# A decoder layer with 32 experts: low halves on VectorE, logits from the raw residual, choice by match-and-replace, first gather ahead of the loop

## The reference, cut to what matters

```python
x = x + hybrid_mixer(rms_norm(x, norm_mix), w_in, ...)      # z = h @ w_in, five column groups of 1024
#   pool: sliding means minus the token, per-group matmul, w_pool_proj
#   lru: width-4 conv, gates (sigmoid), associative scan over the tokens, * gelu(z_gelu), w_lru_proj
#   m = sigmoid(g_a) * y_a + sigmoid(g_b) * y_b;  m @ w_mix_out
memn = rms_norm(mem, norm_mem)
x = x + cross_attention(rms_norm(x, norm_xattn), memn, w_q, w_kv, w_o)
xn = rms_norm(x, norm_moe).reshape(256, 1024)
logits = xn @ w_router + b_router                            # 256 x 32
top_val, top_idx = lax.top_k(logits, 4)
gates = softmax(top_val)
# each expert e: hact = clamped_swiglu(xb @ w_gate_up[e] + b_gate_up[e]); hact @ w_down[e] + b_down[e]
x = x + sum over the chosen experts of gate * expert(xn)
out = rms_norm(x, norm_final)
```

## Time and profile before

| | |
|---|---|
| median of three runs | 1324.38 us |
| profiled execution | 1324.83 us |
| its span, first to last instruction | 1323.0 us |
| mean granted clock of TensorE, share of full | 0.977 |
| TensorE busy | 1204.0 us (91%) |
| VectorE busy | 485.9 us (37%) |
| ScalarE busy | 249.0 us (19%) |
| GpSimd busy | 238.5 us (18%) |
| read from HBM | 459.74 MB, mean 348 GB/s |
| chain that ended last | DMA 51%, PE 41%, DVE 4%, ACT 1% |

### The profile page before, as it was taken

How to read it: one execution, slowest core, us unless ns; L and a number is a source line. 1 busy time by engine, 2 the same in 40 slices (tenths; PEclk the granted TensorE clock), 3 DMA queues, 4 the chain that set the end, 5 groups by cost and what they waited for, 6 DMA issues and landing times.

```text
span 1323.0 us, 18583 instructions
## 1 busy us (share of the span) xinstructions
PE 1204.0 (91%) x7545; PEld 626.3 (47%) x7545; DVE 485.9 (37%) x705; ACT 249.0 (19%) x347; POOL 238.5 (18%) x73
## 2 busy tenths in 40 slices
PE   6996999999969999998899999988999999989996
PEld 6996999998733333333333333333333333333332
DVE  6995976313223322232222222322222223222224
ACT  5427644535320100001000000000000000000002
POOL 5843786976230000000000000000000000000000
PEclk9997989999868999999999999999999999999999
DMA  7533453644968999999999999999999999999991
GB/s 283 188 123 141 146 220 135 220 171 147 350 247 356 429 428 428 429 428 429 429 428 429 428 429 429 429 428 429 429 428 428 429 428 429 428 428 429 429 428 79
DMA packets 36527, 461.25 MB, mean 349 GB/s; under 512 B 4224, under 2 KB 4240, under 8 KB 5392
## 3 DMA queue, kind: packets, MB, share of 16 engines
q1 hardware_dynamic: 36000, 459.82, 83.7%
q0 software_dynamic: 208, 0.54, 0.1%
q10 hardware_dynamic: 288, 0.45, 0.1%
HBM read 459.74 MB, written 1.05 MB: 348 GB/s over the span
## 4 chain that ended last, share of the span: by engine, by line
DMA 51%; PE 41%; DVE 4%; ACT 1%; issue 1%; SPq 0%; DVEq 0%; ACTq 0%
DMA late<-in_w_gate_up 50%; PE ps L1181 17%; PE ps L1064 4%; PE ps L1065 4%; PE ps L1066 4%; PE ps L1083 2%; PE ps L1085 2%; PE ps L1084 2%; PE ps L1099 2%; DVE act_lo L689 1%; PE ps L1232 1%; DVE s L781 1%; PE ps L1206 1%; DMA raw<-in_dense 1%; PE ps L1240 1%
## 5 line engine op out<-in xcount | busy, mean ns | idle before, releaser
L1181 PE MATMUL ps<-late,s 128*64 128x512 f32 x1128 | 517.0, 601 | 65.9 <-DMA late<-in_w_gate_up 64.9
L1182 PE MATMUL ps<-late,s 128*64 128x512 f32 x1128 | 517.0, 601 | 0.0
L1181 PEld LDWEIGHTS ps<-late,s 128*64 128x64 f32 x1128 | 144.0, 137 | 393.5 <-issue 256.3
L370 POOL TENSOR_TENSOR wlo<-raw,whi 128x2048 fp32r<-128x2048 f32 x47 | 225.6, 4812 | 116.1 <-ACT whi L449 116.1
L959 DVE TENSOR_TENSOR res<-res,ps 128x1024 f32<-128x1024 f32 x66 | 80.6, 1221 | 266.7 <-PE ps L1232 266.6
L1064 PE MATMUL ps<-act_hi,whi 128*128 128x256 f32 x576 | 165.5, 287 | 6.8 <-issue 4.6
L1065 PE MATMUL ps<-act_lo,whi 128*128 128x256 f32 x576 | 164.9, 286 | 0.0
L1066 PE MATMUL ps<-act_hi,wlo 128*128 128x256 f32 x576 | 164.7, 286 | 0.0
L1182 PEld LDWEIGHTS ps<-late,s 128*64 128x64 f32 x1128 | 144.0, 137 | 0.0
L598 ACT ACTIVATE s<-ps 128x512 f32<-128x512 f32 x64 | 34.7, 594 | 574.6 <-PE ps L1182 574.6
L1181 PE MATMUL ps<-raw,s 128*64 128x512 f32 x272 | 123.9, 598 | 0.0
(11 more groups left out here) (176 smaller groups left out, 1116.0 us busy)
## 6 DMA issues: line engine op xcount, KB each, us to landing
late<-in_w_gate_up SPq DMA_DIRECT2D x125, 2048.0 KB, 25.5
raw<-in_w_down SPq DMA_DIRECT2D x32, 2048.0 KB, 25.6
raw<-in_dense SPq DMA_DIRECT2D x51, 1024.0 KB, 4.8
late<-in_w_down SPq DMA_DIRECT2D x16, 2048.0 KB, 25.3
s<-in_w_down SPq DMA_DIRECT2D x16, 2048.0 KB, 25.3
raw<-in_w_gate_up SPq DMA_DIRECT2D x2, 2048.0 KB, 8.2
s<-in_w_gate_up SPq DMA_DIRECT2D x1, 2048.0 KB, 13.5
res<-in_x SPq DMA_DIRECT2D x2, 512.0 KB, 5.1
```

Source lines behind the costliest of these rows:

```text
L370: nc.gpsimd.tensor_tensor(wlo[m % SPL][:, :], raw[:, n % RAW, :], whi[m % SPL][:, :].bitcast(F32), ALU.subtract)\
L1181: nc.tensor.matmul(ps[0:SLOTS, bank, :], x_tile, lower, start=start, stop=stop)
L1182: return nc.tensor.matmul(ps[SLOTS:P, bank, :], x_tile, upper, start=start, stop=stop)
```

## The change

1. GpSimd makes no low half of a chunk any more. VectorE makes all 48, each at a place written out in its list (`low_weights(name, j)`: all low halves up to chunk j of that matrix).
2. The last transpose reads the residual itself. The norm's factor `rstd` is applied to the logits when they leave PSUM; the gain goes into the router weights (one multiply on GpSimd). The router weights are the stationary operand (32 columns), in four column tiles of the array, two k-tiles into each; the four partial sums are added by a matmul with four stacked unit matrices (`fold`), which also turns them back.
3. The choice: `match_replace` overwrites the four largest (the other four of the eight are set to a value that is absent), and `pick16` is where the result differs from the logits. `place_or_no` is rank + 1 or 0.
4. `gmat` is made on VectorE from the exponentials of all logits, inside the loop's first round. The three bfloat16 parts are made tile by tile, scaled in the same instruction.
5. `select(0, 0)` stands ahead of the loop on TensorE and VectorE, and ahead of the reading of the number of rounds. The router's three loads stand behind the wait for branch B (`yb_done`) with no low halves ahead of them.

```diff
-            for m, n in enumerate(SPLIT_CHUNKS):                       # GpSimd
...
-                nc.gpsimd.tensor_tensor(wlo[m % SPL][:, :], raw[:, n % RAW, :],
-                                        whi[m % SPL][:, :].bitcast(F32), ALU.subtract)
...
+            nc.gpsimd.tensor_tensor(router_w, router_w, moe_gain, ALU.mult).then_inc(S["router_scaled"], 1)
...
+            square(6, res[:, 0, :], xn_rows[:, 0, :], added_up(0))      # ScalarE
+            high_rows(0)
+            for j in range(3):
+                evacuate("xnT", j, lambda j, b: nc.scalar.activation(
+                    xn_f[:, 2 * j:2 * j + 2, :], two(b), ACT.Copy).then_inc(S["freed_act"], 1))
+            middle_rows(0)
+            evacuate("logitT", 0, lambda j, b: nc.scalar.activation(
+                logit_t, b[:, 0:T], ACT.Copy).then_inc(S["freed_act"], 1))
+            square(7, res[:, 1, :], xn_rows[:, 1, :], added_up(1))
+            high_rows(1)
+            middle_rows(1)
...
+            def low_weights(name, j):                                   # VectorE
+                last = SPLIT_CHUNKS.index(DENSE[name] + j)
+                while next_low[0] <= last:
+                    m = next_low[0]
+                    dve.wait_ge(S["dense_hi_ready"], m + 1)
+                    V.tensor_tensor(wlo[m % SPL][:, :], raw[:, SPLIT_CHUNKS[m] % RAW, :],
+                                    whi[m % SPL][:, :].bitcast(F32), ALU.subtract).then_inc(S["dense_lo_ready"], 1)
+                    next_low[0] += 1
...
             for j in range(4):
                 evacuate("lp", j, merge)
-                if j:
-                    low_of(m_f, "merged", j - 1)
-            low_of(m_f, "merged", 3)
+                low_weights(*(("lp", 3), ("mix", 0), ("mix", 1), ("mix", 2))[j])
+                low_of(m_f, "merged", j)
...
+            for j in range(3):
+                evacuate("o", j, onto_residual)
+            inverse_root(0)
+            evacuate("o", 3, onto_residual)
+            rest_rows_of(0)
+            evacuate("xnT", 3, copied(xn_f))
+            low_rows(0)
+            inverse_root(1)
...
+            link(*[V.match_replace(without[:, t, :], top8[:, 8 * t:8 * t + 8], logit[:, t, :], 2 * ABSENT / 3)
+                   for t in both])
+            V.tensor_tensor(pick16[:], without[:, :, 0:EXPERTS], logit[:, :, 0:EXPERTS], ALU.not_equal)\
+                .then_inc(S["picked"], 1)
+            rest_rows_of(1)
...
-            transposed("xnT", xn_rows, 3)                               # TensorE
+            transposed("xnT", res, lambda t: (S["freed_dve"], evacuated(UNIT["o"] + 2 * t + 1)[1]))
...
+            for kk in range(2):
+                for g in range(GROUPS):
+                    k = 2 * g + kk
...
+                    last = nc.tensor.matmul(b[g * EXPERTS:(g + 1) * EXPERTS, 0:T], router_w[:, k, :], xn_f[:, k, :],
+                                            start=kk == 0, stop=kk == 1)
...
+            pe.wait_ge(S["part_hi"], TT)
+            pe.wait_ge(S["part_mid"], TT)
+            pe.wait_ge(S["part_low"], TT)
+            select(0, 0)
             pe.wait_ge(S["freed_dve"], evacuated(NUNIT - 1)[1])
-            pe.wait_ge(S["part_hi"], 3)
             n = needed_rounds(pe)
             with pe.Fori(0, n) as r:
-                select(r, 0)
                 input_ready(r, 0)
```

More of the change, by code:

```diff
@@ L51 @@
 _at = 0
-for _name, _n in (("ident", P), ("fold", SLOTS), ("before", P), ("ones", P), ("iota", T), ("inv", len(WINDOWS) * PAD)):
+for _name, _n in (("ident", P), ("fold", EXPERTS), ("before", P), ("ones", P), ("iota", T + SLOTS + 1), ("inv", len(WINDOWS) * PAD)):
     CONST[_name] = (_at, _at + _n)
@@ L412, in _, with square @@
             act.dma_start(col[:], cols).then_inc(S["in_cst"], 16)
+            def square(i, src, junk, there):
+                act.wait_ge(*there)
+                nc.scalar.activation(junk, src, ACT.Square, accum_out=ssum[:, i:i + 1]).then_inc(S["squared"], 1)
+                act.wait_ge(S["squared"], i + 1)
+                nc.scalar.activation(root[:, i:i + 1], ssum[:, i:i + 1], ACT.Sqrt, scale=1.0 / D, bias=EPS)\
+                    .then_inc(S["rooted"], 1)
             def squares(n, src, junk, there):
@@ L719, in _ @@
             link(V.memset(u_lru[:, :, 0:PAD], 0.0))
-            units("lrux", 4, lambda j, b: V.tensor_copy(
-                u_lru[:, 2 * j:2 * j + 2, PAD:], two(b)).then_inc(S["freed_dve"], 1))
+            for j in range(4):
+                evacuate("lrux", j, lambda j, b: V.tensor_copy(
+                    u_lru[:, 2 * j:2 * j + 2, PAD:], two(b)).then_inc(S["freed_dve"], 1))
+                low_weights(*(("lrux", 3), ("pool", 0), ("pool", 1), ("pool", 2))[j])
             dve.wait_ge(S["freed_dve"], evacuated(UNIT["lrux"] + 3)[1])
@@ L738, in _ @@
                 if tap < CONV - 1:
+                    low_weights(*(("pool", 3), ("gelu", 0), ("gelu", 1))[tap])
                     dve.wait_ge(S["dve_seq"], seq[0])
@@ L793, in _ @@
             dve.wait_ge(S["freed_act"], evacuated(UNIT["ga"] + 3)[1])
-            units("pp", 4, lambda j, b: V.tensor_tensor(
-                m_f[:, 2 * j:2 * j + 2, :], siga_f[:, 2 * j:2 * j + 2, :], two(b), ALU.mult)
-                .then_inc(S["freed_dve"], 1))
+            for j in range(4):
+                evacuate("pp", j, lambda j, b: V.tensor_tensor(
+                    m_f[:, 2 * j:2 * j + 2, :], siga_f[:, 2 * j:2 * j + 2, :], two(b), ALU.mult)
+                    .then_inc(S["freed_dve"], 1))
+                if j < 3:
+                    low_weights(*(("pp", 3), ("lp", 0), ("lp", 1))[j])
             normalise(1, mem_rows, mem_rows)
+            low_weights("lp", 2)
             def merge(j, b):
@@ L817, in _ @@
             units("mix", 4, onto_residual)
+            low_weights("kb", 0)
             normalise(2, res, xn_rows)
+            low_weights("kb", 1)
             units("ka", 2, copied(k_f))
+            low_weights("q", 0)
             low_from_psum("x1T", "xn", "norm_xattn")
-            units("kb", 2, copied(k_f[:, KT // 2:, :]))
-            units("q", 4, copied(q_f))
+            for j in range(2):
+                evacuate("kb", j, copied(k_f[:, KT // 2:, :]))
+                low_weights("q", 1 + j)
+            for j in range(4):
+                evacuate("q", j, copied(q_f))
+                low_weights(*(("q", 3), ("v", 0), ("v", 1), ("v", 2))[j])
             def maxima(j, b):
@@ L864, in _ @@
-            link(*[V.max_index(idx8[:, 8 * t:8 * t + 8], top8[:, 8 * t:8 * t + 8], logit[:, t, :]) for t in both])
-            link(V.tensor_copy(idxf, idx8[:]))
-            places = iota[:, 0:EXPERTS]
-            link(*[V.tensor_scalar(pick[:, t, :], places, tops(idxf, t, 0), None, ALU.is_equal) for t in both])
-            for j in range(1, TOPK):
-                link(*[V.scalar_tensor_tensor(pick[:, t, :], places, tops(idxf, t, j), pick[:, t, :], ALU.is_equal,
-                                              ALU.add) for t in both])
@@ L891, in _ @@
+            for n in range(2, ROUNDS):
                 link(V.scalar_tensor_tensor(nround, cntmax, float(SLOTS * n), nround, ALU.is_gt, ALU.add))
@@ L972, in _ @@
                 with dve.If(r < 1):
+                    dve.wait_ge(S["gate_exp"], 2 * TT)
+                    dve.wait_ge(S["gmat_zero"], 1)
+                    link(V.reciprocal(grec, gsum))
+                    for t in range(TT):
+                        V.scalar_tensor_tensor(gmat[:, t, 1:EXPERTS + 1], chance[:, t, :], grec[:, t:t + 1],
+                                               pick16[:, t, :], ALU.mult, ALU.mult).then_inc(S["gmat_done"], 1)
                     dve.wait_ge(S["gT_turned"], 1)
@@ L1005, in _ @@
                     add_rows(r, EXPERTS + 1, t)
+                with dve.If(r + 1 < n):
+                    select(r + 1, 0)
                 dve.wait_ge(S["added"], 2 * (r + 1) * BLOCKS + 2)
```

214 lines of the change are left out of this document (101 added, 113 removed).

## The result

| | us |
|---|---|
| before, in the runs beside it | 1324.60 (1324.00 to 1325.34, 4 runs) |
| changed kernel | 1307.39 (1305.38 to 1309.69, 4 runs) |
| ratio | 0.9871, 95% interval 0.9859 to 0.9882 |
| profiled execution, and its span | 1306.64, 1304.7 |

The kernel became 17.2 us faster. The forecast was 4.9 us, and its range began at 1314 us.

A forecast was written before the change was run, and what follows sets the result against it. The weight stream's fixed plateau bounds the kernel: time is the first expert matmul's start plus a constant. +0.2 + 2.7 + 1.7 - 9.45 = -4.85 on 1324.83 gives 1320.0 us profiled, 1319.5 median; range 1314 to 1326.

The forecast's parts named there:

- Around the scans: In gb and pp: scans stay 13.47 us, TensorE's old loss of 8.0 us becomes 8.2, so +0.2 us.
- Rival A: The dense part loses nothing, so -9.45 to -7 us, 1315 to 1317.5 us; chance 17%.
- The merge: At the start of mix: TensorE waits 2.7 us for a bank that VectorE frees, +2.7 us.
- a ring: Serial loop of VectorE and ScalarE in lp's merge: 6.9 us a turn against TensorE's 5.76.
- The clock behind it: After the wait at the start of mix, TensorE's clock falls, costing +1.7 us.
- The routing: From the end of TensorE's o matmuls (E) to first expert matmul: 16.9 us instead of 26.35, gain 9.45 us.
- TensorE's reading of the rounds: Before the first expert matmul: reading the number of rounds follows the gather, taking 1.69 us plus 0.2 hand-over.
- The choice: In the routing, logits to choice: 2.0 us instead of 5.1.
- The column tiles: Router logits: four tiles run concurrently, 1.0 us; 3.8 us if one after another.
- The clock is at half before the first expert matmul in both: Ahead of the first expert matmul: TensorE's clock is at half before and after the change.
- The transfers: Weight queue before the first freed slot: still dry for 5 us, so the gain is not eaten.

The follow-up runs named there:

- The busy GpSimd: Changed kernel plus four unneeded two-input GpSimd subtractions on a spare buffer, from the first multiply ahead of the scans on: 1321.04 us, ratio 0.9971.
- the first experiment: Changed kernel with all low halves but the first back on GpSimd, routing as changed: 1316.93 us, ratio 0.9934.
- the edits of the dense part: Changed kernel with ScalarE's high halves of ga's second and third chunk later, and high weights before merged high rows in the merge: 1293.92 us, ratio 0.9767.
- all three edits: Changed kernel with later ga high halves, high weights before high rows in the merge, and the first gather's semaphore increment ahead of the round count: 1292.91 us.
- the second trace of the changed kernel: The changed kernel itself run once more, nothing altered: 1307.04 us, ratio 0.9863.

## Why the prediction was wrong

**The step that failed** is in *Around the scans*: "scans 13.47 to 154.2". I had just taken the multiplies beside them at their short length, since GpSimd falls silent, and had said that I take all such operations so; but the scans have two SBUF inputs as well, and I kept their long duration. With 4.76 us my own sum gives gb's second low half at 140.7 + 4.8 + 2.3 = 147.8, three microseconds ahead of TensorE, and no new loss. Instead of +0.2 the place brought -8.0. That alone would have put my sum at 1311.8 us for the profiled execution, below the range. The busy GpSimd shows the other side: scans of 11.5 us, and a wait of 6.16 us behind them. Rival A had the direction (nothing lost), but with the old loss still in it; no rival had the old 8.0 us go free.

**Why the old wait stood there** I had not followed to its end: scans, then ScalarE's evacuation of gb, then the high half behind it, then GpSimd's low half, itself slowed by VectorE's multiply. The chain is in the first experiment's rows. The trace of before has the same one: high half from 158.41 to 160.32 us, low half from 160.39 to 166.90 (6.50 us), TensorE at 167.00 in place of 162.38. Both the scans and that low half are long there because GpSimd and VectorE work side by side, and the change shortens both. The same holds of the 0.9 us at pp: the four low halves of activations ahead of it took 15.60 us before and 2.49 now. No run has the one short and the other long on this chain, so how the 4.62 us divide between them is not shown.

**The merge** was right: a ring of 6.8 us (6.9), a wait of 2.5 (2.7). **The clock behind it**, +1.7, was right in size and did not come in the profiled execution: in the eight traces of the table with that wait of 2.4 or 2.5 us, mix to fold takes 133.8 us in four and 135.4 or 135.5 in four, 1.6 apart.

**The routing**: 16.92 us for 16.9, a gain of 9.43 for 9.45, and that it came so near is in part luck. Inside, two misses cancel. The gather started at E + 13.2 in place of 12.2, not because of its operands (ready at 356.7) but of an increment that VectorE gives behind the round count (and ahead of its own reading of it, other than my expectation says); and TensorE's reading of the rounds, which I put 1.7 us behind the gather, lay beside it: x whole and the first matmul follow within 0.97 us, with the gather early, late or in the loop. The choice was faster too: from the logits to it 5.1 us before, 2.0 forecast, 1.9 now (351.33 to 353.19). The column tiles overlap, as forecast: in the first experiment's trace, where the eight logits matmuls found all their inputs ready, they took 1.18 us together at full clock (forecast 1.0, and 3.8 one after another).

```profile
356.13 1.18 PE L1212 MATMUL ps<-s 128*32 128x256 f32 x16 [1.27 <-POOL s L384]
```

"The clock is at half before the first expert matmul in both" held only up to the gather (0.50 in both traces); the pair behind it ran at 1.00 in place of 0.64, 2.0 us that I had not counted.

**The transfers** were right in what came of them, nothing eaten, but not in the margin. I had 5 us without transfers ahead of the first freed slot; it was about 1, since they end some 2.5 us behind the first expert matmul and the pair at full clock frees the slot after 3.69. What the edits of the dense part win is not eaten either, for the last four requests ahead of the loop come earlier with it (344.08 us before, 334.12 now, 320.20 with all three edits). A gain in the routing has no such help, and while the pair runs at full clock there is room for about 1 us more of it.

In the sum: -8.0 for +0.2 in gb and pp (8.2), 2.5 for 2.7 at mix (0.2), -0.4 for 1.7 behind it (2.1), -2.6 for 0 ahead of ga, -2.0 for 0 in the first pair, +1.5 for 0 at the end; together 13.6 us, which but for rounding and 0.1 us outside of the span are the 13.4 between 1320.0 and 1306.64. Of these the first belongs to the change and is shown. The 2.6, 1.7 and 2.0 us come and go between kernels that are identical up to there, by the table above. In two traces of the same kernel only the grp column moved, by 0.9 us. Of the 1.5 at the end the second trace of the changed kernel has 0.6 (from the first w_down request to the output's it is 933.75 us there, 934.66 in the first trace and 933.12 before). The 5 us that the two parts bring only together lie in the same three columns (the low halves alone: 2.0 to 2.9 us later at grp, 130.6 us from mix's first matmul to E in place of 129.0, 2.7 us more in the first pair; the routing alone: 0.7 to 1.5 and, in the first pair, 2.8); whether by chance of single executions or as a lasting effect of the order is not settled.

## What to carry to other kernels

When an engine falls silent, shorten every operation that shared a resource with it, not only the ones beside the edit: go through all rows of that form in the stretch, and ask of each which wait it ends. Follow a wait back past the engine that is named to the operations whose duration made it; here they were GpSimd's low half and, behind ScalarE, VectorE's scans. And before a microsecond or two is won or lost in one trace, look at the granted clock of the same stretch in a trace of another kernel that is identical up to there.

## What the runs showed of the hardware

- VectorE's operations with two SBUF inputs and GpSimd's with SBUF inputs take turns by whole instructions. A scan of 128x256 took 0.66 us or 5.05; the slow ones are as many as GpSimd's operations beside them (2 before, 3 with gb's four low halves on GpSimd). It goes both ways: GpSimd's fourth subtraction of gb took 6.48 us, with a 2.29 us multiply of VectorE ahead of it.
- One SBUF input on GpSimd is enough (multiply by a constant, 5.56 us each: low halves beside it 5.65). Memsets of the same size (1.81 us each) stretched nothing.
- Eight fp32 logits matmuls in four groups of 32 columns took 1.18 us from first to last at full clock with their inputs ready (first experiment), and 2.32 us in the changed kernel, waits for their inputs included. A match-and-replace of 36 elements took 0.18 us and its load 0.09.
- In two executions of the same program TensorE's wait ahead of the end of rx was followed by a clock of 1.00 (after 2.23 us) and by 0.67 (after 2.11 us). In the output matmuls at the end, a wait of 2.15 us was followed by 1.00 before and by 0.55 in the changed kernel.
